# TensorE turns the unit matrix into an unread PSUM bank at the waits of an expert stage

## The reference, cut to what matters

```python
for l in range(DEPTH):                       # 2 layers
    ...                                      # mixer
    # hier_moe: top-1 of 4 groups, then top-2 of the 8 experts in it: 32 experts
    def expert_block(a):
        xb, e = a                            # rows (tokens) of this expert, width 1024
        gate, up = jnp.split(xb @ w_gate_up[e], 2, axis=-1)    # 1024 -> 2 * 512
        return (jax.nn.silu(gate) * up) @ w_down[e]            # 512 -> 1024
```

## Time and profile before

| | |
|---|---|
| median of 3 runs (lowest, highest) | 2137.71 us (2133.04, 2146.65) |
| the profiled execution | 2141.64 us, span 2139.7 us |
| TensorE busy with products | 1692.2 us, 79% of the span |
| VectorE, ScalarE, GpSimd busy | 485.5, 337.0, 121.5 us |
| mean granted TensorE clock | 0.91 |
| HBM traffic | 604.27 MB moved, mean 282 GB/s |

### The profile page before, as it was taken

One profiled execution on the slowest core, in us unless ns is written; L12 is line 12 of the kernel. 1 busy time (PEld: TensorE's weight loads), 2 busy tenths in 40 slices (PEclk: granted clock), 3 DMA queues, 4 the chain that ended last, 5 costly groups with the idle time before them and its releaser, 6 DMA issues.

```text
span 2139.7 us, 25367 instructions
## 1 busy us (share of the span) xinstructions
PE 1692.2 (79%) x8325; PEld 782.5 (37%) x8326; DVE 485.5 (23%) x1022; ACT 337.0 (16%) x665; POOL 121.5 (6%) x147
## 2 busy tenths in 40 slices
PE   5988787688966888888887659998748787887683
PEld 3433343345442434333332324444423333332231
DVE  1679345321140101000000042212410100000003
ACT  3022234222110010101110130001101011111011
POOL 0012000120110000000000010000110000000002
PEclk9999888787977999999999979999879999999996
DMA  9951586686027596999999950200478999999995
GB/s 353 416 177 71 191 322 236 219 290 251 1 112 310 192 415 267 417 419 425 405 421 422 372 196 0 79 0 2 196 278 336 364 419 418 425 422 420 424 420 193
DMA packets 144963, 604.27 MB, mean 282 GB/s; under 512 B 15951, under 2 KB 18288, under 8 KB 128361
## 3 DMA queue, kind: packets, MB, share of 16 engines
q1 hardware_dynamic: 113648, 522.55, 61.4%
q10 hardware_dynamic: 21025, 46.17, 5.7%
q0 software_dynamic: 10208, 34.48, 4.5%
HBM read 551.57 MB, written 52.01 MB: 282 GB/s over the span
## 4 chain that ended last, share of the span: by engine, by line
PE 61%; DMA 16%; DVE 10%; issue 6%; ACT 3%; POOL 1%; SPq 1%; ACTq 1%; DVEq 0%; POOLq 0%
PE ps L921 17%; PE ps L934 10%; PE ps L1046 8%; DMA ring<-in_w_down_dram 8%; PE ps L588 5%; DMA ring<-in_w_gate_up_dram 4%; PE ps L659 3%; PE ps L966 2%; PE ps L688 2%; DVE W L1537 1%; PE ps L944 1%; PE ps L978 1%; PE ps L783 1%; PE ps L533 1%; PE ps L509 1%
## 5 line engine op out<-in xcount | busy, mean ns | idle before, releaser
L921 PE MATMUL ps<-ring,W 128*64 128x512 f32 x2048 | 475.2, 614 | 62.0 <-issue 39.1
L921 PEld LDWEIGHTS ps<-ring,W 128*64 128x64 f32 x2048 | 176.4, 141 | 348.8 <-issue 348.7
L934 PE MATMUL ps<-ring,W 128*64 128x512 f32 x1024 | 256.0, 644 | 57.1 <-DVE W L1860 47.0
L1071 ACT ACTIVATE W<-ps 128x512 f32<-128x512 f32 (+3 forms) x244 | 138.1, 579 | 828.1 <-PE ps L934 349.1
L1854 DVE TENSOR_TENSOR W<-W,ps 128x256 f32<-128x256 f32 x64 | 26.9, 421 | 781.1 <-ACT W L1388 781.1
L1046 PE MATMUL ps<-hT,ring 128*128 128x512 f32 x384 | 167.0, 594 | 0.0
L934 PEld LDWEIGHTS ps<-ring,W 128*64 128x64 f32 x1024 | 87.8, 146 | 184.1 <-issue 183.9
L1046 PEld LDWEIGHTS ps<-hT,ring 128*128 128x128 f32 x384 | 72.4, 190 | 93.9 <-issue 93.9
L688 PE MATMUL ps<-ring,hT 128*128 128x512 f32 x192 | 88.7, 618 | 1.9 <-DVE W L1552 1.9
L1537 DVE SCALAR_TENSOR_TENSOR W<-W,prm 128x512 f32<-128x512 f32 x116 | 85.3, 802 | 0.0
L944 PE MATMUL ps<-C,W 128*128 128x128 f32 x256 | 38.7, 296 | 40.5 <-DMA W<-x_rows 40.5
(11 more groups left out here) (311 smaller groups left out, 1393.6 us busy)
## 6 DMA issues: line engine op xcount, KB each, us to landing
ring<-in_w_gate_up_dram SPq DMA_DIRECT2D x128, 2048.0 KB, 17.3
ring<-in_w_down_dram SPq DMA_DIRECT2D x64, 2048.0 KB, 17.2
ring<-in_w_ada_dram SPq DMA_DIRECT2D x24, 2048.0 KB, 9.5
x_rows<-X ACTq DMA_DIRECT2D x1, 18944.0 KB, 71.2
ring<-in_cache_k_dram SPq DMA_DIRECT2D x64, 256.0 KB, 3.2
W<-x_rows SPq DMA_DIRECT2D x32, 512.0 KB, 16.7
x_rows<-W ACTq DMA_DIRECT2D x128, 128.0 KB, 6.9
ring<-in_cache_v_dram POOLq DMA_DIRECT2D x48, 256.0 KB, 5.1
```

The costliest lines, as they stand in the source:

```text
L921: x = mm(ps[CAP * z:CAP * z + CAP, 2 + j, :], xt[:, k, :], at[:, :, 256 * z:256 * z + 256], start=(k == 0), stop=(k == KD - 1))
L934: x = mm(ps[CAP * z:CAP * z + CAP, 5 + j, :], ht[:, k % 2, CAP * (k // 2):CAP * (k // 2) + CAP], ring[:, 3 * j + 2, at:at + 512], start=(k ...
L1071: return fn(out, src, ACT.Copy, **k)
```

## The change

A helper `fill(n)` on TensorE transposes the unit matrix `ident` n times into the first 128 columns of bank 1. Nobody reads what it writes. It is called in `one_pass` (4, 5 and 3 times, behind the first transposes, the gate and up products and the down products), in `further` (3 times behind each of the three inner loops, by the new argument `between`), and in the steps without `nxt` (6 times behind `gate_up`, 3 times behind `h_turns`). Since bank 1 holds the turned rows of a pair until VectorE has copied them, `one_pass` waits for `xd_ok` too.

```diff
-        def further(eng, l, e, one_pass, ways=(4, 4)):
+        def further(eng, l, e, one_pass, ways=(4, 4), between=None):
...
                             some(ways[1:], at, before)
+                            if between is not None:
+                                between()
...
+                def fill(n):
+                    for _ in range(n):
+                        tr(ps[:, 1, 0:P], ident, ident)
...
                         pe.wait_ge(M["xa_ok"], pdone(l, p))
+                        pe.wait_ge(M["xd_ok"], pdone(l, p))
...
                         x.then_inc(F["products"], 1)
+                        fill(4)
                         pe.wait_ge(F["dve"], c * 4 - 3)
...
                         x.then_inc(F["products"], 1)
+                        fill(5)
                         pe.wait_ge(F["dve"], c * 4 - 2)
...
                         x.then_inc(F["products"], 1)
-
-                    further(pe, l, n, one_pass, ways=(2, 2, 2, 2))
+                        fill(3)
+
+                    further(pe, l, n, one_pass, ways=(2, 2, 2, 2), between=lambda: fill(3))
...
                     if nxt is not None:
                         pair_turns(*nxt)
+                    else:
+                        fill(6)
                     pe.wait_ge(M["h_ok"], done(l, n))
...
                     h_turns(hh[:, j, :], j, M["ht_mm"])
+                    if nxt is None:
+                        fill(3)
                     landed(j, 2, p)
```

## The result

The changed kernel takes 2165.5 us, median of four runs (2155.1 to 2188.3), against 2137.6 for the kernel before; the ratio is 1.0088, 95% interval 1.0052 to 1.0124. Twelve more runs in a later series gave 1.0072 (1.0042 to 1.0102). So the change makes the kernel slower by some 0.7 to 0.9%. The median lies inside the range on record (2118 to 2185) and 24.5 us above the forecast of 2141. By the ratio the result is within the 1% that was given the largest chance (0.69); by the median, above the 2159 us at which "slower by over 1%" began (0.24). The profiled execution has a span of 2153.4 us against 2139.7.

The account below looks back on a forecast made before the run. Weights' DMA was taken to bound the long stretches, TensorE only 390 us of 2140. Fills save 11.9, cost 3.7 in place and 11 through longer code: +2.8 on 2137.7, about 2141 us; range 2118 to 2185.

Parts of the forecast that it names:

- rival 1: Quad loop: each later turn fetches its code anew; 55 to 120 us a layer, priced at 2240 us; chance 0.20.
- What bounds the kernel: Weights' DMA sets the long stretches of both expert stages; TensorE's time counts in only 390 of the 2140 us.
- rival 3: TensorE's time counts everywhere: all 26 slow stretches of the two stages, 44 us, giving 2099 us; chance 0.08.
- What the fills save: Slow stretches of 1.7 us vanish: -8.5 in 654 to 830 us, -1.7 in each of two later stretches; sum -11.9.
- Rival 2: Fills do not hold TensorE's clock, so nothing is saved; about 2152 us; chance 0.14.
- What the fills cost in place: Fills between passes about 2.2 us, behind last passes 1.5 us, none in the steps' gaps; +3.7 (0 to +6).
- What the longer code costs: First-time jumps wait for code: one more stall in the first quads, one in the last, 5.6 us each; +11.
- Over 90 instruction packets, spread over all turns: Sign of rival 1 in the new profile's instruction queue, against 52 or 53 packets if the forecast was right.

Follow-up runs that it names:

- steps only: The changed kernel without the fills in and between the passes, keeping nine in each even step; 2124.9 us, ratio 0.9921; again 2125.9 us, 0.9886.
- the dead-code kernel moved: The kernel before with fills in a never-taken branch, plus 138 long satisfied waits ahead of layer 1's experts; 2158.4 us, ratio 1.0065.
- the kernel moved by 140: The changed kernel with 140 more TensorE instructions, long satisfied waits, ahead of layer 2's first turn; 2142.1 us, ratio 1.0000.
- the kernel moved by 70: The changed kernel with 70 more TensorE instructions, long satisfied waits, ahead of layer 2's first turn; 2224.9 us, ratio 1.0406.
- dead code in the same place: The kernel before with 50 or 56 fills per expert's code in a never-taken branch, loops standing as in the changed kernel; 2182.6 us, ratio 1.0153.

## Why the prediction was right, and where its working was not

The measured time lies in the range because the range took in the mild end of rival 1. The sum itself, +2.8 us, left that effect out, and it priced the longer code inside the first and last quads too high.

**What bounds the kernel** held. From the eighth to the last expert of layer 1 the time is 375.4 us before and 377.5 after: what the fills save on TensorE there buys nothing in this kernel. That rules out rival 3. It is not quite nothing elsewhere: steps only takes 372.1 and 372.2 us there. It also shows where the bound ends: a stretch bound by weights absorbs stalls only up to its slack, and twice 23 us were more than that.

**What the fills save**, -8.5 in the first stretch: measured -8.5 from the first `pair_turns` to the eighth `h_turns`, all six slow groups gone, first-time stalls being in it on both sides (0.71 and 3.91 us before; 3.22 and 2.22 after). That the figures agree is luck: mine was five groups before any cost, the measured one is six, 10.2 us, less the fills' own time and the difference in stalls. Nor is the 180.9 us before a firm base: the dead-code kernel moved, in which no fill runs either, takes 176.4, while the five executions with the changed kernel's layer 1 take 171.7 to 173.5. Rival 2 fell: the clock is 0.98 there, and every `down` and gate and up product of a pass is at 3.65 or 3.66. Which fills do it I had too simple. In the first stretch the `down` that I gave to the steps' fills are fast with the passes' fills alone, and the two slow passes, which I gave to fills of their own, are fast in the kernels without them where no wait for rows stands ahead.

**What the fills cost in place**, +3.7: the pass-to-pass joint costs 0.45 and 0.65 us by the periods, against 0.44 that I took for three fills and double for six; the way out costs 1.53 + 0.63 instead of 2.04, 0.1 us against my 0.3. In the steps nothing. With five joints and five ways out that makes some 3 us, an estimate.

**What the longer code costs**, +11 in one more first-time stall per first quad and one more in a last quad: in the first quad of layer 1 one more long gap, as said, in that of layer 2 none, in the last quad of layer 2 three short gaps (1.54, 3.40 and 0.96 us) for one of 1.97, so that stretch takes 88.4 us instead of 85.9 from the products behind the DMA wait to the last `down`. Without the refetching turns, as in the kernel moved by 140, the sum of all terms is measured at 1.0000 (0.9971 to 1.0029), where I had +2.8 us, 1.001. The extra gap of layer 1 cost nothing by itself: 5.4 us of idle time instead of 4.6, and a slow `gate_up` that lost 1.5 us instead of 2.6. Those of the last quad cost some 5 us, 5.9 of idle time instead of 1.97 and a `gate_up` of 9.79 instead of 8.78, of which the two fast `down` gave 3.4 back. So about half of the +11 came.

**Rival 1, the loop no longer stays loaded**, given 0.20 and priced at 55 to 120 us a layer: it is what happened, in its mild form, in one layer and for two of the six turns, +20.7 us. That is most of the 24.5 us between the forecast and the median; the profiled execution, 2155.1 us, lies only 14 above the forecast. I had taken it as all or nothing for a layer, six turns or none; the kernel moved by 70 shows the full form, 87 us. A turn was priced at 11 to 22 us; two alone cost 24 and 23 on the spot. "Over 90 instruction packets, spread over all turns" was therefore the wrong sign to look for: 71, in two turns.

On this case's measurements a loop over seven packets stays loaded and one over eight may not. The Trainium skill, "Runtime: NRT & Kernel Launch", "Instruction fetch mechanics", gives TensorE 2048 instructions in blocks of 256, first in first out, with the next block fetched ahead; seven and the one behind are just eight, and eighteen packets for two refetched turns of eight are what such an order would give. By that order every turn of a loop over eight would be fetched anew, which only the kernel moved by 70 shows; so the order explains where it can happen and not when. The same section's statement that only two blocks are held does not fit: the kernel before runs a loop of seven packets with no instruction packet from 1640 to 2020 us.

**Left open:** why, over eight packets, one turn refetches and another does not; why dead code in the same place refetched in layer 1, where the fills did not, and whether it does so in each execution; and what makes the products of a pass run at 5.35 us.

## What to carry to other kernels

Count instructions before adding "free" work to a loop on an engine: here idle time was filled for some 3 us, and the place of the loop that the 206 instructions in each turn made longer cost more than the fills saved. Here a loop over seven packets was safe and one over eight was not, so its place counts as much as its length; the DMA queue of the instructions and the gaps named issue show it, and 140 instructions of padding in an idle stretch undid it. Fill the few waits that lose the clock, and check whether the later ones still lose it before filling them too: the kernel with 38 of the 206 instructions is 1.8% faster than the one with all, part of it by luck of position.

## What the runs showed of the hardware

- TensorE idles 2.0 to 4.2 us in most gaps that I put down to a first-time jump, and 8.8 to 12.7 us where a refetched turn of the loop begins. The `gate_up` behind mostly runs 8.4 to 10.1 us instead of 7.07, with the granted clock fallen, as in the second `gate_up` of the changed kernel's third turn (window of the trace, columns as above):

```profile
1743.40:1746.40 3.00, 3.00 (x8) 1.06 (x10) 0.00 (x0) 0.00 (x0) 0.00 (x0) 0.50 0.81 287
```

- Turning a unit matrix holds the granted clock (0.98 over the first stretch) and also raises it: behind 14 fills of 3.25 us the eight turns of layer 2 took 1.30 us and the `gate_up` 7.09, instead of 1.95 and 9.44.
- Two programs with loops of 1686 and 1688 instructions, by the count in the same place, kept or lost their code in different turns of their profiled executions.
